# Two-block transformer kernel on one core: the last weight unit by blocks with its sums of squares taken early, down projections' and gates' low parts on VectorE alone, and a norm's next low part in two halves

## The chip, the cores and the metric

One core of one Trainium2 chip. The metric is device time in microseconds (us) of one launch. The time before is the median of three runs; one further execution was recorded by the hardware profiler, and every row below is from that one.

## The reference, cut to what matters

Two decoder blocks on 256 tokens (272 with 16 meta tokens) of width 1024, in float32. The first has two layers: attention with low-rank projections, then a mixer of window means, each followed by a feed-forward part with a causal convolution over 3 tokens. The second is gated linear attention with a short convolution, a gated feed-forward part, and a gate on a per-layer embedding. What matters here:

```python
def conv_ffn(h, w_up, conv_w, conv_b, w_down):
    u = h @ w_up                       # 1024 -> 2 x 2816
    u = conv_b + sum(conv_w[j] * up[:, j:j + L] for j in range(3))
    gate, val = jnp.split(u, 2, axis=-1)
    return (jax.nn.silu(gate) * val) @ w_down      # 2816 -> 1024
...
h = h + rmsnorm(f, norm_ffn_post[i])
...
        u2 = _rmsnorm(h, ln2_g[i])
        a, bb = jnp.split(u2 @ w_gate_upffn[i], 2, axis=-1)
        h = h + (jax.nn.silu(a) * bb) @ w_down[i]
        u3 = _rmsnorm(h, ln3_g[i])
        gate = jax.nn.sigmoid(u3 @ w_ple_gate[i])
        h = h + gate * (p[i] @ w_ple_proj[i])
    return _rmsnorm(h, lnf_g)
```

## The kernel before, in words

Activations lie transposed: the 1024 channels are 8 chunks of 128 partitions, tokens are the columns (272, 258 or 256 of them). Every float32 product is three matmuls of rounded parts, high x high, low x high and high x low (lines 441 to 443), which add up in one PSUM bank.

Weights come as a fixed list of units (`STREAM`). A unit is 16 to 24 tiles of 128x128 and yields 1 to 8 blocks of 128 output channels. Unit n uses slot n % 2 of three pairs of buffers: `raw` (filled by DMA on SyncE's queue), `wh` and `wl`. Its life is: SyncE loads `raw` when both low parts of unit n - 2 are written (`slot_free`); ScalarE copies raw to `wh` (`high`, lines 956 and 959) when TensorE is through with unit n - 2; then `wl` = raw - wh is made (`low`). VectorE makes the first `vector_cols(n)` columns (lines 1317 and 1323) and GpSimd, if `pool_share(n)`, the rest (line 1832), a quarter of the tiles rounded up. TensorE waits for all of it (`parts_ready`). Each engine runs its own list of instructions in order, written out by hand; semaphores tie them together.

Some units are made in two halves: `high(n, first=...)` and `low(n, first=...)` split at `first_half(n)`, half of VectorE's columns, and TensorE, given `first_low`, starts the unit on the first half and waits for the rest when it reaches it. During the last up units the second unit of a down projection is made so (on VectorE the order is first half, `x_low` of the last chunk of the hidden vector at line 1431, second half).

A norm works on sums of squares. ScalarE squares a chunk (line 977 or 967), GpSimd adds chunks into `acc` (line 1849), TensorE multiplies `acc` and the last one or two squares by a column of 1/1024 (lines 509, 512, 529: `norm_sums`, `chunk_sums`), a small chain on VectorE (or square root on ScalarE at line 983 and reciprocal at 1341) gives 1/rms, and TensorE spreads it over the partitions (line 543, `norm_rows`). Where a projection follows a norm, its first unit runs on values not yet divided, and the rows are spread in the middle of its second unit.

After each layer part `add_post` on VectorE adds the normed result to `h` chunk by chunk, makes the low part of the next operand (`u_low`, line 1332) and at the end calls `low(unit)` for the second weight unit that follows: one instruction over 2048 columns. TensorE is by then in the first unit of the next part.

The program's end: eight units `down2` (one block of 22 tiles each), then four units `pgate` (two blocks each). For each pair of blocks VectorE scales them by the rows out of PSUM (`scaled`, line 1379), ScalarE takes the sigmoid (line 1298), VectorE multiplies by the projected embedding (line 1810) and adds to `h` (line 1812), ScalarE squares `h` (line 977) and GpSimd adds squares 0 to 5. Then come the last norm (six plus two squares), eight VectorE products (line 1818) and four stores. `keep_busy` multiplies weights into a bank that nobody reads, to pass the time of a wait.

## Time and profile before

| what | us |
|---|---|
| median of three runs | 948.71 (945.36 to 949.46) |
| the profiled execution, its own time | 950.01 |
| its span, first to last instruction | 948.2 |
| TensorE matmul busy in it | 912.0 |
| VectorE, ScalarE, GpSimd busy in it | 681.7, 512.9, 276.4 |

Times in rows are us from the span's start. A row of the timeline has start, length, engine, line, operation and tiles; the bracket is the engine's idle time just before it and what ended it. "issue" there means that the profile names no releaser. A matmul's row is longer than the distance between two rows, since matmuls are pipelined.

### The profile page before, as it was taken

What the parts mean: (1) busy time and instruction counts of PE and PEld (TensorE: products, weight loads), DVE (VectorE), ACT (ScalarE), POOL (GpSimd) and SP (SyncE); (2) the same over time, 40 slices, a digit from 0 to 9 for tenths busy, and PEclk for the clock granted to TensorE, in tenths of its full rate; (3) what the DMA queues carried; (4) which work ended last, traced back from release to release, by engine and by line L of the source; (5) the groups of instructions that cost most, each with busy time, mean ns of one, the idle gap of its engine ahead of it and who ended that gap; (6) DMA issues with size and microseconds to landing.
All of it is one profiled execution on the core that took longest, in us unless ns stands there. A gap on an engine that the chain in (4) does not pass through costs nothing.

```text
span 948.2 us, 19994 instructions
## 1 busy us (share of the span) xinstructions
PE 912.0 (96%) x7354; PEld 884.7 (93%) x7354; DVE 681.7 (72%) x1168; ACT 512.9 (54%) x851; POOL 276.4 (29%) x202
## 2 busy tenths in 40 slices
PE   6999999999999999999999999999989999999996
PEld 6986798999999997899999999999989999999995
DVE  7767529999994225699999533889777888785666
ACT  5765656666655346566666544454455554454443
POOL 4118752000015534200000464200024334345633
PEclk9999999999999998799999999999999999999997
DMA  7541132544554531144445554354234555465431
GB/s 249 181 158 46 46 134 89 178 177 177 177 196 164 210 133 46 45 177 177 177 177 210 184 188 174 96 194 157 89 113 174 185 201 182 177 227 184 166 134 45
DMA packets 22147, 146.80 MB, mean 155 GB/s; under 512 B 2752, under 2 KB 5328, under 8 KB 6736
## 3 DMA queue, kind: packets, MB, share of 16 engines
q1 hardware_dynamic: 22096, 146.11, 43.1%
q8 instruction: 34, 0.56, 0.2%
q14 instruction: 17, 0.14, 0.0%
HBM read 143.94 MB, written 1.05 MB: 153 GB/s over the span
## 4 chain that ended last, share of the span: by engine, by line
PE 83%; DVE 10%; ACT 3%; issue 2%; POOL 1%; DMA 0%; POOLq 0%; SPq 0%; DVEq 0%; ACTq 0%
PE bank L441 23%; PE bank L442 23%; PE bank L443 23%; PE bank L681 2%; DVE u_low L1332 2%; ACT w_high L959 1%; DVE w_low L1323 1%; PE bank L529 1%; DVE h L1405 1%; PE bank L814 1%; DVE bank L1397 1%; PE bank L697 1%; PE bank L543 1%; PE bank L715 1%; PE bank L512 1%
## 5 line engine op out<-in xcount | busy, mean ns | idle before, releaser
L441 PE MATMUL bank<-u_high,w_high 128*128 128x256 f32 (+2 forms) x1400 | 401.7, 287 | 13.1 <-DVE u_low L1332 8.6
L442 PE MATMUL bank<-u_low,w_high 128*128 128x256 f32 (+2 forms) x1400 | 399.4, 285 | 0.0
L443 PE MATMUL bank<-u_high,w_low 128*128 128x256 f32 (+2 forms) x1400 | 398.2, 284 | 0.0
L1832 POOL TENSOR_TENSOR w_low<-raw,w_high 128x512 fp32r<-128x512 f32 (+1 forms) x60 | 168.8, 2814 | 463.0 <-ACT w_high L959 463.0
L1323 DVE TENSOR_TENSOR w_low<-raw,w_high 128x1024 fp32r<-128x1024 f32 (+5 forms) x119 | 198.1, 1664 | 125.7 <-ACT w_high L959 124.6
L441 PEld LDWEIGHTS bank<-u_high,w_high 128*128 128x128 f32 x1400 | 266.1, 190 | 15.5 <-DVE u_low L1332 8.1
L442 PEld LDWEIGHTS bank<-u_low,w_high 128*128 128x128 f32 x1400 | 265.8, 190 | 0.0
L443 PEld LDWEIGHTS bank<-u_high,w_low 128*128 128x128 f32 x1400 | 265.5, 190 | 0.0
L959 ACT ACTIVATE w_high<-raw 128x1024 fp32r<-128x1024 f32 (+5 forms) x119 | 195.2, 1640 | 73.2 <-PE bank L443 65.0
L441 PE MATMUL bank<-x_high,w_high 128*128 128x256 f32 (+1 forms) x608 | 173.9, 286 | 4.4 <-ACT x_high L1261 2.5
L443 PE MATMUL bank<-x_high,w_low 128*128 128x256 f32 (+1 forms) x608 | 173.3, 285 | 0.0
L442 PE MATMUL bank<-x_low,w_high 128*128 128x256 f32 (+1 forms) x608 | 172.7, 284 | 0.0
L441 PEld LDWEIGHTS bank<-x_high,w_high 128*128 128x128 f32 x608 | 115.3, 190 | 6.4 <-issue 3.3
L442 PEld LDWEIGHTS bank<-x_low,w_high 128*128 128x128 f32 x608 | 115.2, 189 | 0.0
L443 PEld LDWEIGHTS bank<-x_high,w_low 128*128 128x128 f32 x608 | 115.1, 189 | 0.0
L956 ACT ACTIVATE w_high<-raw 128x1024 fp32r<-128x1024 f32 (+1 forms) x66 | 65.7, 995 | 77.1 <-PE bank L443 73.6
L1454 DVE SCALAR_TENSOR_TENSOR conv_out<-conv_in,par,conv_out 128x272 f32<-128x272 f32 (+1 forms) x176 | 82.2, 507 | 7.6 <-ACT conv_out L1036 2.0
L1849 POOL TENSOR_TENSOR acc<-acc,sq 128x256 f32<-128x256 f32 (+1 forms) x51 | 45.0, 883 | 141.1 <-ACT sq L977 130.6
L1317 DVE TENSOR_TENSOR w_low<-raw,w_high 128x1024 fp32r<-128x1024 f32 (+1 forms) x66 | 75.5, 1143 | 12.2 <-ACT w_high L956 9.1
L1379 DVE TENSOR_TENSOR conv_in<-bank,r_rows 128x256 f32<-128x256 f32 (+2 forms) x140 | 54.1, 427 | 15.0 <-PE bank L443 9.6
L1043 ACT ACTIVATE conv_out<-conv_out 128x272 f32<-128x272 f32 (+1 forms) x44 | 18.7, 425 | 71.1 <-DVE conv_out L1454 71.1
L1036 ACT ACTIVATE conv_out<-conv_in,par 128x272 f32<-128x272 f32 (+1 forms) x88 | 48.1, 594 | 11.8 <-DVE conv_in L1379 10.7
(213 smaller groups left out, 1030.1 us busy)
## 6 DMA issues: line engine op xcount, KB each, us to landing
raw<-w_up_dram SPq DMA_DIRECT2D x66, 1024.0 KB, 4.8
raw<-w_down_dram SPq DMA_DIRECT2D x24, 1408.0 KB, 6.1
raw<-w_gin_c_dram SPq DMA_DIRECT2D x4, 1536.0 KB, 6.8
raw<-w_wo_dram SPq DMA_DIRECT2D x4, 1024.0 KB, 5.0
raw<-w_wout_dram SPq DMA_DIRECT2D x4, 1024.0 KB, 4.9
raw<-w_pgate_dram SPq DMA_DIRECT2D x4, 1024.0 KB, 4.7
raw<-w_gin_v_dram SPq DMA_DIRECT2D x2, 1024.0 KB, 4.7
raw<-w_gin_g_dram SPq DMA_DIRECT2D x2, 1024.0 KB, 6.2
```

The lines of the kernel that those rows point to most:

```text
L441: nc.tensor.matmul(out, hi, rhi, start=start, stop=False)
L442: nc.tensor.matmul(out, hi, rlo, start=False, stop=False)
L443: return nc.tensor.matmul(out, lo, rhi, start=False, stop=stop)
L956: nc.scalar.activation(wh[n % 2][:, 0:split], raw[n % 2][:, 0:split], ACT.Copy).then_inc(*S.step(first))
L959: nc.scalar.activation(wh[n % 2][:, split:cols], raw[n % 2][:, split:cols], ACT.Copy).then_inc(high_parts, 1)
L1036: nc.scalar.activation(cv[:, hf, 0:T], ur[:, hf, 2 + skip:2 + skip + T], ACT.Identity, bias=pcol(f"cb{l}", hf * FC + j), scale=pcol(f"cw{l ...
L1317: nc.vector.tensor_tensor(wl[n % 2][:, 0:split], raw[n % 2][:, 0:split], wh[n % 2][:, 0:split].bitcast(F32), ALU.subtract)\
L1323: nc.vector.tensor_tensor(wl[n % 2][:, split:cols], raw[n % 2][:, split:cols], wh[n % 2][:, split:cols].bitcast(F32), ALU.subtract).then_i ...
L1379: nc.vector.tensor_tensor(out, bank[BLOCKS[b]["bank"]][:, 0:T], rows[:, 0:T], ALU.mult)\
L1454: nc.vector.scalar_tensor_tensor(cv[:, hf, 0:T], ur[:, hf, skip + tap:skip + tap + T], pcol(f"cw{l}", (tap * 2 + hf) * FC + j), cv[:, hf, ...
L1832: nc.gpsimd.tensor_tensor(wl[n % 2][:, at], raw[n % 2][:, at], wh[n % 2][:, at].bitcast(F32), ALU.subtract).then_inc(low_parts_g, pool_cou ...
L1849: nc.gpsimd.tensor_tensor(acc[:, a, 0:T], acc[:, a, 0:T], x, ALU.add).then_inc(*step)
```

## The change

Five edits. (1) `pool_share` no longer holds for `down0`, `down1`, `down2` and `pgate`: VectorE makes their whole low part; `first_half` follows from the wider `vector_cols` (1408 columns of 2816 in place of 1024), and SyncE's queue writes four loads of each down projection out ahead of its loop instead of two. (2) `add_post` makes the next unit's low part in two instructions of 1024 columns with a signal each, and TensorE starts `up0`'s, `up1`'s and `gin`'s second unit on the first. (3) In the gates ScalarE makes the high part and VectorE the low part of the last unit one turn earlier, during the first pair of blocks. (4) The last unit runs block after block. In the middle of its second block TensorE takes the sum over squares 0 to 3; squares 4 to 7 are multiplied singly, from a buffer of their own each (`m`), so that GpSimd adds four squares instead of six; six unread matmuls stand before the last one and four after it. (5) In the last pair each block goes through scaling, sigmoid, product, addition and square by itself, and the table for the square root is loaded after the last square.

```diff
@@ -85,7 +85,8 @@
 PIECES = DC // 2
 
 
-SQUARES_IN_M = {"f0": T1, "a1": T1, "f1": SEQ + HISTORY, "g": SEQ}
+
+SQUARES_IN_M = {"f0": T1, "a1": T1, "f1": SEQ + HISTORY, "g": SEQ, "out": SEQ}
 
 OVER_D, OVER_Q, OVER_KV, OVER_HEAD = range(4)
 MEAN_OF = (D, QR, KVR, GDV)
@@ -143,8 +144,10 @@
 def pool_share(n):
 
 
-    return n == FIRST_UNIT["up0"] or UNITS[n]["name"] not in ("uqn", "uqr", "uk", "uv", "up0", "up1", "gin_k", "gin_v",
-                                                               "gin_g", "gin_c", "wout", "pproj")
+
+    return n == FIRST_UNIT["up0"] or UNITS[n]["name"] not in ("uqn", "uqr", "uk", "uv", "up0", "down0", "up1", "down1",
+                                                               "gin_k", "gin_v", "gin_g", "gin_c", "wout", "pproj",
+                                                               "down2", "pgate")
 
 
 def pool_counts(n):
@@ -366,7 +369,7 @@
                                 sp.dma_start(dst, src_).then_inc(tables_in, 16)
                 else:
 
-                    apart = 4 if not pool_share(n0 + 2) else 2 if units == DC or not pool_share(n0 - 1) else 0
+                    apart = 4 if not pool_share(n0 + 2) else 2 if not pool_share(n0 - 1) else 0
                     for u in range(apart):
                         slot_free(n0 + u, pool_share(n0 + u - 2))
                         sp.dma_start(raw[(n0 + u) % 2][:, 0:cols], src[u, :, :]).then_inc(loaded[(n0 + u) % 2], 16)
@@ -554,6 +557,12 @@
                     nc.tensor.matmul(bank[BLOCKS[b]["bank"]][:, 0:T1], wh[n % 2][:, 0:P], wh[n % 2][:, 0:T1],
                                      start=True, stop=True)
 
+            def spare_products(n, times):
+
+
+                for _ in range(times):
+                    nc.tensor.matmul(bank[2][:, 0:T1], wh[n % 2][:, 0:P], wh[n % 2][:, 0:T1], start=True, stop=True)
+
             def keep_busy_early(n):
 
 
@@ -585,7 +594,8 @@
                 us = (uh, ul)
                 unit(n0, T, us, high_then_low(sums_name))
                 norm_sums(sums_name, f"{sums_name} acc {DC - 2}", squares(0, T), True)
-                unit(n0 + 1, T, us, None, lambda: norm_rows(sums_name, token_rows(R_BANK, T)))
+                unit(n0 + 1, T, us, None, lambda: norm_rows(sums_name, token_rows(R_BANK, T)),
+                     first_low=f"{sums_name} next low" if l < 2 else None)
                 with pe.Fori(0, (FC - 2) // 2) as i:
                     for k in range(2):
                         unit(n0 + 2 + k, T, us, i=i)
@@ -855,7 +865,7 @@
             us = (uh, ul)
             unit(n, T, us, high_then_low("g"))
             norm_sums("g", f"g acc {DC - 2}", squares(0, T), True)
-            unit(n + 1, T, us, None, lambda: norm_rows("g", token_rows(R_BANK, T)))
+            unit(n + 1, T, us, None, lambda: norm_rows("g", token_rows(R_BANK, T)), first_low="g next low")
             pe.wait_ge(freed["v"], BLOCKS[FIRST_BLOCK["gin_a"]]["freed"])
             pe.wait_ge(tables_in, 16 * 7)
             for pair in range(2):
@@ -933,8 +943,13 @@
             norm_sums("e", f"e acc {DC - 2}", squares(0, T), True)
             unit(n + 1, T, us, None, lambda: norm_rows("e", token_rows(R_BANK, T)))
             unit(n + 2, T, us)
-            unit(n + 3, T, us)
-            norm_sums("out", f"out acc {DC - 3}", squares(0, T), True, late=(DC - 2, DC - 1))
+            blocks_in_turn(n + 3, T, lambda b, k: (uh[:, k, 0:T], ul[:, k, 0:T]), DC,
+                           middle=lambda: norm_sums("out", f"out acc {DC - 5}", squares(0, T), True, late=()))
+            for k in range(DC - 4, DC - 1):
+                chunk_sums("out", len(squares(0, T)), k)
+            spare_products(n + 3, 6)
+            last_sums("out", len(squares(0, T)))
+            spare_products(n + 3, 4)
             norm_rows("out", token_rows(R_BANK, T))
 
 
@@ -1290,17 +1305,29 @@
                 u_high("e", c, T, META, "ln3")
             for u in range(4):
                 n = FIRST_UNIT["pgate"] + u
-                if n + 2 < len(UNITS):
+                if u == 0:
                     high(n + 2)
-                for b in range(2):
+                def gate(b):
                     c = 2 * u + b
                     act.wait_ge(freed["v"], BLOCKS[FIRST_BLOCK["pgate"] + c]["freed"])
                     nc.scalar.activation(cv[:, b, 0:T], cv[:, b, 0:T], ACT.Sigmoid).then_inc(*S.step(f"ple gate {c}"))
-                if u == 3:
-                    load_table(ACT.Sqrt)
-                for c in range(2 * u, 2 * u + 2):
+
+                def out_square(b):
+                    c = 2 * u + b
                     act.wait_ge(*done(f"out h {c}"))
                     square("out", c, h[:, c, META:T1], T, S.step(f"out sq {c}"))
+                if u == 3:
+                    for b in range(2):
+                        gate(b)
+                        out_square(b)
+                else:
+                    gate(0)
+                    gate(1)
+                    if u == 0:
+                        high(n + 3)
+                    out_square(0)
+                    out_square(1)
+            load_table(ACT.Sqrt)
             rms("out", 2)
 
 
@@ -1408,7 +1435,12 @@
                         scale(c + 1)
                     if c > 1:
                         u_low(nxt, c - 1, T, t0, gain)
-                low(unit)
+
+                half, cols, at = first_half(unit), vector_cols(unit), unit % 2
+                dve.wait_ge(high_parts, unit + 1)
+                for cs, signal in ((slice(0, half), S.step(f"{nxt} next low")), (slice(half, cols), (low_parts_v, 1))):
+                    nc.vector.tensor_tensor(wl[at][:, cs], raw[at][:, cs], wh[at][:, cs].bitcast(F32), ALU.subtract)\
+                        .then_inc(*signal)
 
             def ffn_up(l, T, conv, name, skip=0):
 
@@ -1800,17 +1832,23 @@
             keep_rows("e", T)
             for u in range(4):
                 n = FIRST_UNIT["pgate"] + u
-                for b in range(2):
+
+                def gate_in(b):
                     scaled(cv[:, b, 0:T], FIRST_BLOCK["pgate"] + 2 * u + b, (freed["v"], 1), T)
-                if u == 1:
-                    low(n + 2)
-                for b in range(2):
+
+                def gated(b):
                     c = 2 * u + b
                     dve.wait_ge(*done(f"ple gate {c}"))
                     nc.vector.tensor_tensor(cv[:, b, 0:T], cv[:, b, 0:T], m[:, c, 0:T], ALU.mult).then_inc(*S.step())
                     dve.wait_ge(*S.now())
                     nc.vector.tensor_tensor(h[:, c, META:T1], h[:, c, META:T1], cv[:, b, 0:T], ALU.add)\
                         .then_inc(*S.step(f"out h {c}"))
+
+                for step, b in ((gate_in, 0), (gated, 0), (gate_in, 1), (gated, 1)) if u == 3 else \
+                        ((gate_in, 0), (gate_in, 1), (gated, 0), (gated, 1)):
+                    step(b)
+                if u == 0:
+                    low(n + 3)
                 dve.wait_ge(*S.now())
             norm("out", tiles_of(T))
             dve.wait_ge(*done("out rows"))
@@ -1840,7 +1878,7 @@
             def add_square(name, c, T, ready, a=0, k=None):
                 label = c if k is None else k
                 pool.wait_ge(*ready)
-                if name in SQUARES_IN_M:
+                if name in SQUARES_IN_M and name != "out":
 
                     pool.wait_ge(*done(f"{name} u low {c}"))
                 pool.wait_ge(*S.now())
@@ -1936,7 +1974,7 @@
             low(FIRST_UNIT["pgate"] + 2)
             low(FIRST_UNIT["pgate"] + 3)
             clear("e")
-            for c in range(DC - 2):
+            for c in range(DC - 4):
                 add_square("out", c, T, done(f"out sq {c}"))
```

## Rows read from the trace of the kernel before

**Rows 1.** The page: busy times of the engines.

```profile
PE 912.0 (96%) x7354; PEld 884.7 (93%) x7354; DVE 681.7 (72%) x1168; ACT 512.9 (54%) x851; POOL 276.4 (29%) x202
```

**Rows 2.** Busy time by stretch: the last down projection and the end, with its columns.

```profile
core 0: us, PE busy (x) PEld busy (x) DVE busy (x) ACT busy (x) POOL busy (x), PEclk, DMA share, GB/s
860.00:910.00 50.00, 50.00 (x425) 50.00 (x424) 29.43 (x20) 18.92 (x18) 30.80 (x14) 1.00 0.47 167
936.00:948.20 12.20, 3.91 (x18) 3.45 (x18) 5.53 (x15) 3.02 (x7) 0.73 (x1) 0.58 0.25 86
```

**Rows 3.** TensorE's timeline: second unit's first matmul behind the first and third norm.

```profile
154.39 0.37 PE L441 MATMUL bank<-u_high,w_high 128*128 128x272 f32 x1 [0.56 <-issue]
...
603.82 0.36 PE L441 MATMUL bank<-u_high,w_high 128*128 128x256 f32 x1 [0.50 <-issue]
```

**Rows 4.** VectorE's timeline: the low part behind the first of these norms.

```profile
151.43 2.85 DVE L1323 TENSOR_TENSOR w_low<-raw,w_high 128x2048 fp32r<-128x2048 f32 x1
```

**Rows 5.** Groups by line and shape: count, busy us and mean ns, idle before.

```profile
L1832 POOL TENSOR_TENSOR w_low<-raw,w_high 128x768 fp32r<-128x768 f32 x26 | 94.5, 3633 | 320.2 <-ACT w_high L959 320.2
L1323 DVE TENSOR_TENSOR w_low<-raw,w_high 128x2048 fp32r<-128x2048 f32 x33 | 77.8, 2358 | 89.4 <-ACT w_high L959 89.4
...
L1317 DVE TENSOR_TENSOR w_low<-raw,w_high 128x1024 fp32r<-128x1024 f32 x46 | 56.3, 1224 | 4.3 <-ACT w_high L956 1.2
```

**Rows 6.** TensorE's timeline: waits at the starts of the down projections.

```profile
298.71 0.39 PE L441 MATMUL bank<-x_high,w_high 128*128 128x272 f32 x1 [0.19 <-POOL w_low L1832]
...
530.67 0.36 PE L441 MATMUL bank<-x_high,w_high 128*128 128x256 f32 x1 [0.19 <-DVE x_low L1431]
...
534.20 0.36 PE L441 MATMUL bank<-x_high,w_high 128*128 128x256 f32 x1
...
539.94 0.38 PE L441 MATMUL bank<-x_high,w_high 128*128 128x256 f32 x1 [0.54 <-POOL w_low L1832]
...
847.40 0.36 PE L441 MATMUL bank<-x_high,w_high 128*128 128x256 f32 x1 [0.63 <-issue]
```

**Rows 7.** VectorE's and GpSimd's timelines at these starts.

```profile
530.10 0.42 DVE L1431 TENSOR_TENSOR x_low<-x_full,x_high 128x256 fp32r<-128x256 f32 x1
...
844.29 2.87 POOL L1832 TENSOR_TENSOR w_low<-raw,w_high 128x768 fp32r<-128x768 f32 x1 [4.25 <-ACT w_high L959]
```

**Rows 8.** Timelines at the start of the gates: VectorE, GpSimd, TensorE.

```profile
913.84 1.52 DVE L1332 SCALAR_TENSOR_TENSOR u_low<-h,par,u_high 128x256 fp32r<-128x256 f32 x1
...
912.21 2.87 POOL L1832 TENSOR_TENSOR w_low<-raw,w_high 128x512 fp32r<-128x512 f32 x1 [4.08 <-ACT w_high L959]
...
915.51 0.36 PE L441 MATMUL bank<-u_high,w_high 128*128 128x256 f32 x1 [0.45 <-DVE u_low L1332]
```

**Rows 9.** Timelines before the last unit: ScalarE, GpSimd, TensorE.

```profile
925.01 1.90 ACT L959 ACTIVATE w_high<-raw 128x2048 fp32r<-128x2048 f32 x1
...
926.99 2.85 POOL L1832 TENSOR_TENSOR w_low<-raw,w_high 128x512 fp32r<-128x512 f32 x1 [7.17 <-ACT w_high L959]
...
930.05 0.36 PE L441 MATMUL bank<-u_high,w_high 128*128 128x256 f32 x1 [0.78 <-issue]
```

**Rows 10.** Timelines of the end: VectorE and GpSimd beside each other, ScalarE, TensorE.

```profile
932.37 0.76 DVE L1379 TENSOR_TENSOR conv_out<-bank,r_rows 128x256 f32<-128x256 f32 x2
...
930.24 3.58 POOL L1849 TENSOR_TENSOR acc<-acc,sq 128x256 f32<-128x256 f32 x4
...
936.89 1.28 ACT L986 ACT_TABLE_LOAD   x1
...
940.65 0.17 ACT L983 ACTIVATE norm_t<-bank 128x2 f32<-128x2 f32 x1 [1.65 <-PE bank L529]
...
941.14 1.22 PE L543 MATMUL bank<-ident,norm_y 128*128 128x128 f32 x4 [0.53 <-DVE norm_y L1341]
```

**Rows 11.** Busy time by stretch, columns as in rows 2: around the second norm.

```profile
381.00:389.00 8.00, 8.00 (x43) 8.00 (x43) 3.41 (x10) 4.05 (x8) 1.06 (x2) 0.57 0.00 1
398.50:402.00 3.50, 3.50 (x17) 3.50 (x18) 3.26 (x10) 0.15 (x1) 0.00 (x0) 0.51 0.66 246
```

## The prediction, made before the change was timed

> **What bounds the kernel now.** I read the page's busy times first: TensorE is busy in 912.0 of 948.2 us, the others 682 at most [rows 1]. So only two things can move the end: how long TensorE waits, and the tail after its last product. In the stretches the reader sees that the last down projection has no waits at all, 425 matmuls in 50.0 us, 0.118 each, while from 936.0 to the end TensorE works 3.9 of 12.2 us [rows 2]. Then the timeline of TensorE for its waits, and the other engines' timelines around each wait for its cause. A wait costs more than its bracket: a full-rate matmul's row is 0.28 long but starts 0.12 after the one before, so idle time x costs x + 0.16, and the next row comes 0.1 late. I count x + 0.25 behind a product and x + 0.1 behind the short sums of a norm.
>
> **The norms' halves (edit 2).** The first product of the second unit waits 0.56 us behind the first norm, 0.58 behind the second, 0.50 behind the third [rows 3]. The bracket names nobody, but VectorE's low part of 2048 columns runs from 151.43 to 154.28 [rows 4], and TensorE starts 0.1 after it. It takes 2.85 where such a part takes 2.36 on average; an instruction of 1024 columns takes 1.22 [rows 5]. So the first half is ready at 151.43 + 0.5 + 1.2 = 153.2, before the sums end (about 153.8), and the wait is gone: (0.56 + 0.58 + 0.50) + 3 x 0.1 = 1.9 us. The second half is ready at about 154.35, and TensorE comes to it 24 matmuls later (3 us). The extra instruction costs VectorE under 0.1, which moves the norm's small chain by as much; its rows are asked for only in mid-unit. `up0` and `up1` then run with TensorE as the bound, and the third gain goes into a stage whose VectorE chain starts from the rows that TensorE spreads, so it starts earlier too. If it does not, 0.6 is lost: 1.3 to 1.9.
>
> **Low parts of the down projections (edit 1).** Removed: GpSimd's 768 columns, 3.63 us on average beside VectorE's 2.36 for 2048 [rows 5]. Added: VectorE does 2816. From 1.22 at 1024 and 2.36 at 2048 a column costs 1.1 ns, so 3.1 to 3.2 us. The unit's low part is then ready 0.5 us and more before, and at `down0` and `down1` these waits go: 0.19 + 0.25 = 0.4 (at 298.71); 0.54 + 0.25 = 0.8 (at 539.94) [rows 6]; at 534.20 the first half now reaches three chunks further, 0.3; a like one in `down0` 0.15. At 847.40 the row says "issue", but GpSimd's part ended at 844.29 + 2.87 = 847.16 [rows 7]. VectorE alone: its first half waits for ScalarE's longer one and ends about 844.3, then the hidden product, then 1408 columns (1.6) to about 846.5; TensorE is free at 846.6. The gain is 0.63 + 0.25 = 0.9; if VectorE is 0.3 late, 0.6. Against it: at `down0` and `down1` the first half on VectorE grows from 1024 to 1408 columns, +0.4 us, ahead of `x_low`, which ended at 530.52 [rows 7] and for which TensorE already waited (530.67, [rows 6]). That costs 0.4 in each, 0.8 together. ScalarE's longer first half is hidden by the wait for VectorE behind it. Sum: 0.15 (`down0`) + 0.7 (`down1`) + 0.9 = 1.8; between 1.2 and 2.6 (`x_low` hidden). In the units' middle nothing changes, as TensorE has no wait there [rows 2]; ScalarE 2.6 and VectorE 3.2 after a slot comes free make 6.0 of a unit's 66 x 0.118 = 7.8. SyncE's two more loads written out ahead of the loop wait for the same slots, which come free earlier: nothing. The squares that GpSimd adds come sooner: nothing.
>
> **Start of the gates (edit 1).** The last low part of `h` took 1.52 us instead of about 0.5 because GpSimd was at its 2.87 us part, and TensorE waited 0.45 [rows 8]. Now VectorE's part takes 2.3 from 912.17, then 0.5: ready at 914.9 instead of 915.36, and the wait costs 0.2 instead of 0.7. Gain 0.5.
>
> **Last unit earlier (edit 3).** TensorE waits 0.78 at 930.05, until GpSimd's part ended at 926.99 + 2.85; ScalarE had begun the high part at 925.01, behind two blocks' sigmoids and squares [rows 9], though TensorE had left that slot 48 x 0.118 = 5.7 before 929.3, at 923.6. Now (the old times less 0.5): high part 923.2 to 925.1, low part to 927.45, TensorE ready for it at 930.05 - 0.78 - 0.16 - 0.5 = 928.6. The stall, 1.0, is gone for TensorE. What is queued behind: VectorE's scaling of blocks 2 and 3, which frees the banks that the last unit needs now stands behind this low part; done at 927.9 and 928.2, before 928.6. That works because scaling reads PSUM: two of them took 0.76 with GpSimd's additions running beside [rows 10]. The Trainium skill says so too (SBUF — State Buffer, Who interferes with whom): a VectorE instruction with one SBUF input does not contend with GpSimd, one with two is fully blocked until the other has finished. The row agrees; if the scaling were blocked, the banks would come 0.8 later and 0.4 of the gain would be gone.
>
> **The tail (edits 4 and 5).** Now VectorE's chain decides, not TensorE, so I step through it from 927.45, with 0.42 a step on VectorE or ScalarE and 0.05 a hand-over. Blocks 2, 3: scaling 0.8, a block by GpSimd's second addition until 929.0, four steps, 930.7. Blocks 4, 5: scaling 0.8, sigmoid, 0.5 behind GpSimd, four steps, 933.9. Block 6: scaling, sigmoid, product, addition, 935.7. Block 7, whose product is long ready (TensorE ends at about 935.0, with 0.7 for the sums in the middle): scaling 936.1, sigmoid 936.55, two steps 937.5, square 937.9. Then the table, 1.28 as before [rows 10], which formerly ran beside VectorE's last products, now lies on the path: 939.3 with its small trial instruction. Sums of square 7 end at about 938.4, hidden, and so are the ten unread matmuls (1.3). The square root starts at 939.3 where it started at 940.65 [rows 10]: 1.35 gained from the gates' start to here, the 0.5 and what survives of the 1.0 in it. Spreading the rows took 1.22 at a mean clock of 0.58 [rows 2, 10]; at full clock it is about 0.6, so 0 to 0.6 more, of which I take none, because TensorE is idle for two stretches of a microsecond there now too. The eight products and four stores are unchanged. Bounds: 0.6 (GpSimd blocks four steps, not two) and 2.4.
>
> **Sum.** 1.9 + 1.8 + 1.35 = 5.05 us. Against the profiled execution, 950.01 (span 948.2 and 1.8 around it): 945.0. That execution lies 1.3 above the median of the three runs, so the median goes from 948.71 to 943.7, 0.53% less. Bounds: 3.1 to 6.9.
>
> **Rivals.**
> A, chance 0.18: TensorE's clock gives back more. Behind the second norm the clock was at its lower level (1.2 of 2.4 GHz) for 3.5 us and TensorE began 17 matmuls there where about 29 fit [rows 11]; before it TensorE had paced itself by `u_low` and then had the wait of rows 3. The norms before and after look alike and had no such stretch, so the removed 0.7 may be enough. Gain 1.5 more, and with full clock in the tail 2: 941.8. Against it: the longer drop before it, 8 us at 0.57, lies where nothing is changed [rows 11]. The Trainium skill (TensorE: Matmul & The Clock Gate, Part 1) says the halved rate is the default and activity lifts it, which would favour this rival; no row here shows a stall of that size deciding.
> B, 0.22: the end gives back its gain. Edit 3 puts 2.3 us of VectorE ahead of six blocks' work, and edit 5 puts the table behind the last square. If GpSimd's four additions each block VectorE for their full 0.9 us (3.58 for four, [rows 10]), the square root starts a microsecond later: gain 0.3 there, 4.0 in all, 944.7.
> C, 0.14: TensorE's removed waits in the norms or at the down projections return one step later (the third norm's in the `gin` stage, `x_low` 0.4 later than thought in both down projections): 1.4 less, 945.1; with B as well 946.2.
> D, 0.04, slower: clock drops move. One more long one (43 matmuls in 8 us where about 65 fit, [rows 11]) costs some 2.7; two eat the 5.05 and leave 949.1, three 951.8. It decides from the second. For it: one VectorE instruction less or more moves every later stretch, and the three runs already span 4.1 us. Against it: every edit makes TensorE denser but the last one.
> E, 0.02: the change does nothing, since the waits are replaced one by one: 948.7.
> My forecast as worked out: 0.40.
>
> **How the numbers follow.** 0.5% of 948.71 is 4.7 us, about what a measurement of this kernel can tell from no change; the line is at 944.0. The forecast lies 0.3 past it, so its 0.40 split 0.30 faster and 0.10 same; A is faster, 0.18; B and C mostly same, 0.06 of their 0.36 faster; D slower in 0.03 of 0.04, E same. Faster 0.54, same 0.43, slower 0.03. The range takes A at its far end (941.8 less 1.3 for the spread of the runs) and C with B at the other (946.2 with 0.8): 940.5 to 947.0.
>
> **What would show it.** Right: no idle row of TensorE behind the norms; none at the second and third unit of `down1` or at the start of `down2`; the wait for `x_low` in `down1` at 0.6 instead of 0.19, and a new one in `down0`; low parts of 2816 columns at 3.1 to 3.2 us; TensorE going into the last unit without a wait; the chain of waits ending over VectorE's steps, the table load, the square root. Wrong: a wait for a free bank at the last unit, a wait for GpSimd's fourth sum in the middle of it, or TensorE waiting for the second half at the third chunk of the second unit.

## The result, and the profile after

| | before | changed |
|---|---|---|
| median, us | 948.71 (945.36 to 950.51, 5 runs) | 939.38 (937.44 to 940.41, 5 runs) |
| profiled execution, span | 948.2 | 938.6 |

The medians differ by 9.3 us. The ratio is 0.9895 (95% interval 0.9872 to 0.9918); it is an estimate over all runs, here and below, and not the quotient of the two medians. The forecast was 943.7 with a range from 940.5, so the sign was right and the size was too small by almost half.

The page of the changed kernel, its busy times and the granted clock in 40 slices:

```profile
PE 909.2 (97%) x7372; PEld 883.9 (94%) x7372; DVE 684.6 (73%) x1172; ACT 512.1 (55%) x851; POOL 191.6 (20%) x172
...
PEclk9999999999999998899999999999999999999998
```

TensorE's busy time falls by 2.8 us although it runs 18 matmuls more; GpSimd loses 85 us of work and VectorE gains 3 [rows 1]. A fall in busy time with more matmuls points to the clock. Busy time by stretch behind the first and the second norm (columns as in [rows 2]):

```profile
152.00:159.00 7.00, 7.00 (x60) 6.96 (x60) 6.63 (x16) 2.33 (x5) 0.33 (x1) 1.00 0.45 152
...
395.00:398.50 3.50, 3.50 (x31) 3.45 (x31) 3.22 (x12) 1.64 (x2) 0.33 (x1) 1.00 0.24 56
```

Behind the second norm TensorE has 31 matmuls in 3.5 us at full clock, where before it had 17 at half [rows 11]. TensorE's timeline: first matmul of the second unit behind the first norm, the last chunk of `down1`'s first unit, and the second unit behind the third norm:

```profile
153.42 0.39 PE L444 MATMUL bank<-u_high,w_high 128*128 128x272 f32 x1
...
525.71 0.29 PE L446 MATMUL bank<-x_high,w_low 128*128 128x256 f32 x1
526.01 0.36 PE L444 MATMUL bank<-x_high,w_high 128*128 128x256 f32 x1
...
596.86 0.37 PE L444 MATMUL bank<-u_high,w_high 128*128 128x256 f32 x1
```

None of these rows has a bracket, as those of [rows 3, 6] had; only the last chunk of `down1`'s first unit starts 0.30 behind its neighbour instead of 0.12, and there TensorE had waited in [rows 6] too. In the stages around `down0` and `down2` no matmul starts more than 0.2 behind the one before. VectorE at the start of the gates and before the last unit:

```profile
904.33 2.29 DVE L1350 TENSOR_TENSOR w_low<-raw,w_high 128x2048 fp32r<-128x2048 f32 x1 [1.58 <-ACT w_high L974]
906.54 0.48 DVE L1359 SCALAR_TENSOR_TENSOR u_low<-h,par,u_high 128x256 fp32r<-128x256 f32 x1
...
917.35 2.29 DVE L1350 TENSOR_TENSOR w_low<-raw,w_high 128x2048 fp32r<-128x2048 f32 x1 [1.29 <-ACT w_high L974]
```

`u_low` takes 0.48 instead of 1.52 [rows 8]. The last unit's low part finds VectorE idle for 1.29 us in front of it. ScalarE at the end:

```profile
929.25 0.42 ACT L982 ACTIVATE m<-h 128x256 f32<-128x256 f32 x1 [0.95 <-DVE h L1844]
929.68 1.28 ACT L1001 ACT_TABLE_LOAD   x1
930.97 0.20 ACT L1001 ACTIVATE warm<-ident 128x1 f32<-128x1 f32 x1
931.08 0.15 ACT L998 ACTIVATE norm_t<-bank 128x2 f32<-128x2 f32 x1
```

The table load stands on the path, as forecast.

**Where the 9.6 us of the span went.** I cut each trace at the starts of the same high parts on ScalarE (a fixed list of instructions) and compared the pieces. "Start" runs from the span's start to the third high part, "end" from the third last one to the span's end; pieces that differ by 0.1 or less everywhere are left out.

| piece | before | changed | gain |
|---|---|---|---|
| start | 10.9 | 10.6 | 0.3 |
| first norm and first turns of `up0` | 16.6 | 16.0 | 0.6 |
| `up0` to `down0` | 32.6 | 31.5 | 1.1 |
| second norm and first turns of `up1` | 33.2 | 31.1 | 2.1 |
| `up1` to `down1` | 31.8 | 30.2 | 1.6 |
| end of `down1`, third norm, first units of `gin` | 31.4 + 30.2 | 31.2 + 29.1 | 1.3 |
| `up2` to `down2` | 26.7 | 25.8 | 0.9 |
| end | 38.0 | 36.3 | 1.7 |

The start is not the change's: no edit touches it, and it takes 10.0 to 10.9 in the profiles of this document, 10.0 in a run whose code is there the same as before.

### The profile page after: what moved, and what is told of

It reads as the page before. It is cut to its first block, busy times and chain, and to the rows that moved or that the text cites. A ratio compares the mean times of both kernels' runs of the same rounds, so it can differ in the third digit from the quotient of the medians.

```text
span 938.6 us, 19945 instructions
## 1 busy us (share of the span) xinstructions
PE 909.2 (97%) x7372; PEld 883.9 (94%) x7372; DVE 684.6 (73%) x1172; ACT 512.1 (55%) x851; POOL 191.6 (20%) x172
## 4 chain that ended last, share of the span: by engine, by line
PE 86%; DVE 8%; ACT 3%; issue 1%; DMA 1%; SPq 0%; DVEq 0%; ACTq 0%
PE bank L444 24%; PE bank L445 24%; PE bank L446 24%; PE bank L691 2%; PE bank L532 1%; PE bank L824 1%; ACT w_high L974 1%; DVE u_low L1359 1%; PE bank L707 1%; DVE h L1432 1%; DVE bank L1424 1%; PE bank L546 1%; PE bank L482 1%; DVE w_low L1350 1%; PE bank L515 1%
## 5 line engine op out<-in xcount | busy, mean ns | idle before, releaser
L1350 DVE TENSOR_TENSOR w_low<-raw,w_high 128x1024 fp32r<-128x1024 f32 (+6 forms) x115 | 205.7, 1788 | 112.2 <-ACT w_high L974 111.2
L1887 POOL TENSOR_TENSOR acc<-acc,sq 128x272 f32<-128x272 f32 (+1 forms) x45 | 53.2, 1181 | 511.7 <-ACT sq L992 502.1
L971 ACT ACTIVATE w_high<-raw 128x1024 fp32r<-128x1024 f32 (+2 forms) x66 | 67.5, 1023 | 72.8 <-PE bank L446 69.2
L1870 POOL TENSOR_TENSOR w_low<-raw,w_high 128x512 fp32r<-128x512 f32 (+1 forms) x32 | 70.6, 2206 | 141.7 <-ACT w_high L974 141.7
L1344 DVE TENSOR_TENSOR w_low<-raw,w_high 128x1024 fp32r<-128x1024 f32 (+2 forms) x66 | 77.9, 1180 | 13.4 <-ACT w_high L971 10.9
L1486 DVE SCALAR_TENSOR_TENSOR conv_out<-conv_in,par,conv_out 128x272 f32<-128x272 f32 (+1 forms) x176 | 79.2, 490 | 7.5 <-ACT conv_out L1051 2.0
```

The source lines that it names most:

```text
L971: nc.scalar.activation(wh[n % 2][:, 0:split], raw[n % 2][:, 0:split], ACT.Copy).then_inc(*S.step(first))
L1344: nc.vector.tensor_tensor(wl[n % 2][:, 0:split], raw[n % 2][:, 0:split], wh[n % 2][:, 0:split].bitcast(F32), ALU.subtract)\
L1350: nc.vector.tensor_tensor(wl[n % 2][:, split:cols], raw[n % 2][:, split:cols], wh[n % 2][:, split:cols].bitcast(F32), ALU.subtract).then_i ...
L1486: nc.vector.scalar_tensor_tensor(cv[:, hf, 0:T], ur[:, hf, skip + tap:skip + tap + T], pcol(f"cw{l}", (tap * 2 + hf) * FC + j), cv[:, hf, ...
L1870: nc.gpsimd.tensor_tensor(wl[n % 2][:, at], raw[n % 2][:, at], wh[n % 2][:, at].bitcast(F32), ALU.subtract).then_inc(low_parts_g, pool_cou ...
L1887: nc.gpsimd.tensor_tensor(acc[:, a, 0:T], acc[:, a, 0:T], x, ALU.add).then_inc(*step)
```

## The experiments

Before each stands what was expected of it. Times are medians; the pieces are those of the table. "The root" is the square root of the last norm. The kernel before was run beside each group: 947.74, 947.75 and 948.92.

**One low part behind the norms again.** Edit 2 undone:

```diff
-                half, cols, at = first_half(unit), vector_cols(unit), unit % 2
-                dve.wait_ge(high_parts, unit + 1)
-                for cs, signal in ((slice(0, half), S.step(f"{nxt} next low")), (slice(half, cols), (low_parts_v, 1))):
-                    nc.vector.tensor_tensor(wl[at][:, cs], raw[at][:, cs], wh[at][:, cs].bitcast(F32), ALU.subtract)\
-                        .then_inc(*signal)
+                low(unit)
```

and `first_low` taken from the three second units.

> The changed kernel with edit 2 alone undone: the low part behind a norm is one instruction of 2048 columns again, and TensorE waits for all of it. The forecast's term: 1.9 us slower than the changed kernel (941.3), by waits of 0.5 to 0.6 us at three places. Theory (the removed wait behind the second norm also kept TensorE's clock up there): 3.4 slower (942.8) in executions in which a stretch at the lower clock follows the second norm, and such a stretch is in the profile. Rival (the three gains are lost again one stage later): no slower than 939.4, with the three waits there but an equally long idle time gone elsewhere.

943.04 (6 runs), 3.7 over the changed kernel; ratio to before 0.9934 (0.9908 to 0.9961). Its busy times by stretch, behind the second and behind the first norm:

```profile
397.20:400.60 3.40, 3.40 (x19) 3.40 (x18) 2.87 (x6) 0.00 (x0) 0.00 (x0) 0.50 0.88 308
154.80:158.20 3.40, 3.40 (x17) 3.40 (x16) 2.92 (x6) 0.00 (x0) 0.00 (x0) 0.51 0.89 306
```

Both stretches are at the lower level, 1.2 GHz. The piece of the second norm is 33.2 again against 31.1: by the run with the wait filled, below, 0.6 of the 2.1 is the wait and 1.5 the clock. The rival, gains lost again one stage later, falls.

**GpSimd's share back in the down projections.** Edit 1 undone for `down0`, `down1` and `down2` (the three names taken out of the list in `pool_share`):

> The changed kernel with edit 1 undone for the three down projections alone: GpSimd makes 768 of 2816 columns again. Forecast's term: 1.8 us slower (941.2): waits of 0.4, 1.1 and 0.9 back, x_low 0.4 sooner in two places. Theory (GpSimd's 2.8 us part in the last up turns blocks VectorE's taps, which makes x_low later, not sooner): 3.3 slower (942.7), x_low of the last chunk some 1.2 us later than in the changed kernel and a tap of about 2.1 us instead of 0.5 in the turn before. Rival (the gain behind the up units is the clock's): under 1 slower.

942.46 (8 runs), 3.1 over the changed kernel; ratio to before 0.9932 (0.991 to 0.9955). The pieces are 32.7, 31.8 and 26.7 against 31.5, 30.2 and 25.8: 3.7 us, twice the forecast's 1.8. The rival (the gain is the clock's, under 1 us) falls. Why, in three timelines of the last turn but one of `up0`. Before, GpSimd and VectorE:

```profile
278.22 2.81 POOL L1832 TENSOR_TENSOR w_low<-raw,w_high 128x768 fp32r<-128x768 f32 x1 [126.08 <-ACT w_high L959]
...
279.25 2.08 DVE L1454 SCALAR_TENSOR_TENSOR conv_out<-conv_in,par,conv_out 128x272 f32<-128x272 f32 x1
```

The changed kernel, VectorE:

```profile
277.43 1.62 DVE L1350 TENSOR_TENSOR w_low<-raw,w_high 128x1408 fp32r<-128x1408 f32 x1
278.97 0.50 DVE L1486 SCALAR_TENSOR_TENSOR conv_out<-conv_in,par,conv_out 128x272 f32<-128x272 f32 x1
```

This experiment, VectorE:

```profile
278.63 2.08 DVE L1485 SCALAR_TENSOR_TENSOR conv_out<-conv_in,par,conv_out 128x272 f32<-128x272 f32 x1
```

A tap of the convolution (one multiply-add over a chunk) takes 2.08 us where 0.50 is its length: it starts in the middle of GpSimd's 2.81 us part and ends 0.3 after it. Counted from the start of the piece, `x_low` of the last chunk but one then starts 0.9 us later than in the changed kernel in both `down0` and `down1`, and that of the last chunk 0.5 later, not the 1.2 expected: VectorE's shorter first half gives some of it back. At `down2` GpSimd's part blocks `x_low` itself, 2.06 us instead of 0.42 in both last turns. That is the rule of exclusive access that the prediction cites for the last unit (the Trainium skill, SBUF — State Buffer, Who interferes with whom: of two such instructions the later one is blocked until the other has finished). This trace agrees with it within 0.2 us: 1.6 us of block behind a part that had 1.8 to run.

**The end undone.** Edits 3, 4 and 5 taken back, the gates' low parts still on VectorE:

> The changed kernel with edits 3, 4 and 5 undone: the last unit's parts one turn later, both blocks together, sums at the end, table load ahead of the last squares; the gates' low parts stay on VectorE. Forecast's term, 1.35 less the 0.5 of the gates' start: 0.85 slower (940.3). Theory (as the changed kernel's trace reads, 1.8 from the gates' start on, 0.5 of it from the start): 1.3 slower (940.7). Rival (the low part on VectorE alone already gives the last unit in time): TensorE goes into the last unit with a wait under 0.3 and the time is 0.5 slower or less.

938.69 (6 runs), no slower than the changed kernel at 939.38 (0.9898, 0.9871 to 0.9925, beside 0.9895). The rival holds. VectorE's low part of the last unit and TensorE behind it:

```profile
915.72 2.29 DVE L1333 TENSOR_TENSOR w_low<-raw,w_high 128x2048 fp32r<-128x2048 f32 x1 [1.50 <-ACT w_high L969]
...
923.70 0.28 PE L446 MATMUL bank<-u_high,w_low 128*128 128x256 f32 x1
...
926.81 0.37 PE L532 MATMUL bank<-mean_weights,sq 128*128 128x1 f32 x1 [1.83 <-ACT sq L987]
```

The low part ends at 918.01 and TensorE goes into the last unit at 918.1 with no idle row: VectorE's 2.29 us are in time even one turn later, if only by 0.1, and only GpSimd's 2.85 had been late [rows 9]. The end piece is 36.5 against 36.3 (0.3 before rounding). In this profile the clock fell just before the last norm's sums; what that hides is under "The gates' low parts alone".

**Down projections alone.** The kernel before with only the three `down` names added to `pool_share`'s list:

> The kernel before with only the low parts of the three down projections given to VectorE. Forecast's term: 1.8 us faster than before (946.9). Theory (VectorE no longer blocked by GpSimd in the last up turns): 3.3 faster (945.4). Rival (the parts depend on each other, and alone this one only moves the wait to x_low): no faster than before by 0.5. The half-clock stretch behind the second norm should still be in the profile by the theory on the clock, as the wait there is still made.

945.07 (12 runs): 0.9971 (0.995 to 0.9992), 2.7 faster. In the profile the three pieces are 31.5, 30.2 and 25.8, as in the changed kernel, 3.6 together. The two pieces behind `down1` and around the third norm are 31.2 and 29.8 instead of 31.4 and 30.2: another 0.6 that this edit alone gives. A half-clock stretch of 3.4 us stands behind the second norm, as expected, and one behind the first.

**A down projection's first half at 1024 columns.**

```diff
-            return vector_cols(n) // P // 2 * P
+            return 8 * P if UNITS[n]["name"].startswith("down") else vector_cols(n) // P // 2 * P
```

> The changed kernel with the first half of a down projection's low part at 1024 columns, as before, and all of it still on VectorE. It measures the cost that the forecast put at 0.4 us in each of the first two down projections: VectorE's first half 1.22 instead of 1.62 us, x_low of the last chunk 0.4 earlier. If TensorE waits for x_low in the changed kernel, its start of the down projection is 0.4 shorter in each (0.8 in all); if not, as its trace reads (one start 0.18 late, in down1, none in down0), the gain is 0.1 to 0.25 in down1 and nothing in down0, and the time is 939.2 beside 939.4.

939.71 (4 runs), 0.9916 (0.9885 to 0.9947): no difference. The pieces are 31.5 and 30.2 as in the changed kernel. The last `x_low` starts 0.27 sooner than in the changed kernel and nothing is gained by it. So the 0.4 us that the forecast put on each of two starts is not there: `x_low` has room.

**The last unit in two halves.** `high(n + 3, first="last first high")` on ScalarE and `low(n + 3, None, "last first high")` on VectorE:

> The changed kernel with the last unit's high and low parts in two halves, so that VectorE starts 0.9 us sooner on it and is through 0.8 sooner. If VectorE's list is what sets the end from there on, the stretch from the last high part to the end is 0.5 to 0.8 shorter (bounded by TensorE's last product, which VectorE then meets earlier). Rival (the table load and the sums set it): no shorter by more than 0.1.

937.82 (4 runs), 0.9899 (0.9867 to 0.9931). To compare ends without the clock I count from the first matmul that spreads the rows of the gates' norm. The last low part ends at 7.0 instead of 7.8 and block 6 is added 0.8 sooner, but the last addition to `h` ends at 17.2 instead of 17.3 and the square root starts at 19.1 instead of 19.2. The rival's number holds (no more than 0.1), by a cause that it did not name: TensorE's last product ends at 15.4 in both and now bounds the last block.

**The last unit's parts in their old turn.** Edit 3 undone, 4 and 5 kept:

```diff
-                if u == 0:
+                if n + 2 < len(UNITS):
                     high(n + 2)
...
-                    if u == 0:
-                        high(n + 3)
```

and on VectorE `low(n + 2)` in the second turn, between scaling and products.

> The changed kernel with edit 3 alone undone: the last unit's parts one turn later, as before, with edits 4 and 5 kept. Theory, from the run with all three undone (the end took 36.5 us from the third last high part on, against 36.3): edit 3 costs 0.7, because VectorE stands idle for 1.3 us in front of a high part that cannot come sooner, with two blocks' scaling behind it, and edits 4 and 5 gain 0.9. So this one ends 0.4 to 0.7 sooner than the changed kernel, 35.7 in that stretch, and TensorE goes into the last unit with a wait under 0.2. The forecast's view (edit 3 removes a wait of 1.0): a wait of 0.8 to 1.0 in front of the last unit and the end 0.3 or more later.

937.97 (6 runs), 0.9899 (0.9873 to 0.9925). Counted as above, the fourth block is added at 10.3 instead of 10.8, so edit 3 does cost VectorE 0.5 there, but the square root starts at 19.1 instead of 19.2, and the end piece is 36.2; TensorE has no idle row in front of the last unit. The wait of 0.8 to 1.0 that the forecast's view asks for does not come; my 0.4 to 0.7 does not come either, for the bound is again TensorE's last product at 15.4, which the sums in the middle of the unit put 0.65 later than without them (14.7).

**The norms' waits filled.** Edit 2 undone and, for the first two norms, added work: five matmuls that nobody reads between the sums and the second unit.

```diff
+                if l < 2:
+                    pe.wait_ge(high_parts, n0 + 2)
+                    for _ in range(5):
+                        nc.tensor.matmul(bank[3 * (n0 % 2) + 2][:, 0:T1], wh[(n0 + 1) % 2][:, 0:P],
+                                         wh[(n0 + 1) % 2][:, 0:T1], start=True, stop=True)
```

> The changed kernel with edit 2 undone and, at the first two norms, five matmuls that nobody reads in the wait between the sums and the second unit (added work: TensorE is busy there and the second unit starts no sooner). Theory on the clock: the waits still cost 0.6 us each, but no stretch at the lower clock follows the first or the second norm, so the stage behind the second norm takes 31.7 us instead of 33.2 (31.1 with edit 2 in place) and that behind the first is never 1.5 longer. Rival (the lower clock came from something else, such as VectorE's later instructions): the stage takes 33.2 and the half-clock stretch is there.

941.18 (8 runs), 0.9935 (0.9912 to 0.9957). Busy times behind the second and behind the first norm:

```profile
396.50:400.00 3.50, 3.50 (x32) 3.45 (x31) 3.26 (x9) 2.45 (x4) 0.33 (x2) 1.00 0.13 19
154.00:157.50 3.50, 3.50 (x18) 3.50 (x18) 3.23 (x12) 0.37 (x1) 0.06 (x1) 0.51 0.61 206
```

Behind the second norm the clock stays up and the piece is 31.7, as expected (the wait kept, the clock not lost): the wait is 0.6 of the 2.1 and the clock 1.5. Behind the first norm the stretch at the lower level is there all the same. Half of the expectation fails, so filling the wait is not sufficient.

**The table ahead of the last square.** The run with edit 3 undone, and `load_table(ACT.Sqrt)` moved between the last sigmoid and the last square:

> Edit 3 undone and edits 4 and 5 kept, as in the run before, and the table for the square root loaded between the last sigmoid and the last square. Counted from the first matmul that spreads the rows of the gates' norm, the square root starts at 19.1 us there. If the table load lies on the path behind the last square, it starts 0.3 to 0.5 sooner, at 18.6 to 18.8. Rival (the last square then waits for the table and the sums come later by as much): at 19.1 again.

938.23 (4 runs), 0.9901 (0.9879 to 0.9924). The square root starts at 18.85 instead of 19.1: 0.25, a little under the expectation.

**The end together.** That, with the last unit's parts in halves in their old turn, three unread matmuls instead of six, and the sums over squares 0 to 3 behind the unit:

```diff
-            blocks_in_turn(n + 3, T, lambda b, k: (uh[:, k, 0:T], ul[:, k, 0:T]), DC,
-                           middle=lambda: norm_sums("out", f"out acc {DC - 5}", squares(0, T), True, late=()))
+            blocks_in_turn(n + 3, T, lambda b, k: (uh[:, k, 0:T], ul[:, k, 0:T]), DC)
+            norm_sums("out", f"out acc {DC - 5}", squares(0, T), True, late=())
```

> All that the runs point to at the end: edit 3 undone, the last unit's parts in two halves in their turn, the sums over squares 0 to 3 after the last unit and not in its middle (0.65 us less ahead of the last product), three unread matmuls instead of six, the table ahead of the last square. The square root starts at 18.0 to 18.3 us from the rows of the gates' norm, against 19.2 in the changed kernel, and the end is 0.9 to 1.2 sooner: some 938.3 beside 939.4. If VectorE's list for the earlier blocks still holds it back, under 0.5.

937.71 (5 runs), 0.9899 (0.988 to 0.9917). ScalarE's timeline:

```profile
925.60 1.28 ACT L1001 ACT_TABLE_LOAD   x1
926.89 0.20 ACT L1001 ACTIVATE warm<-ident 128x1 f32<-128x1 f32 x1
927.00 0.40 ACT L982 ACTIVATE m<-h 128x256 f32<-128x256 f32 x1
928.09 0.17 ACT L998 ACTIVATE norm_t<-bank 128x2 f32<-128x2 f32 x1 [0.70 <-PE bank L532]
```

The table load is hidden beside VectorE's last two steps and the square root starts at 18.15, 1.06 sooner than in the changed kernel; the end piece is 35.4 against 36.3. By the root this end is the best of all here; by the medians (interval of the ratio inside that of the changed kernel) it can't be told from it.

**Norms' halves alone.** The kernel before with edit 2:

> The kernel before with edit 2 alone. Theory: no stretch at the lower clock behind the first and the second norm, the stage behind the second takes 31.1 us instead of 33.2, and those behind the first and third are 0.6 to 0.7 shorter: 3.4 us in all, 4.9 where before had a stretch behind the first norm too: 944 to 945.5. The forecast's term alone, 1.9: 946.8.

944.51 (10 runs), 0.996 (0.9945 to 0.9976), 4.4 faster; the piece of the second norm 31.1, no stretch at the lower level behind either norm.

**The gates' low parts alone.** The kernel before with `pgate` added to the list:

> The kernel before with only the gates' low parts given to VectorE. Theory: the wait of 0.78 us in front of the last unit goes by this alone, not by moving the low part: the square root starts at 19.5 us from the rows of the gates' norm instead of 20.4, and the last low part of h is 0.5 sooner: 1.4 in all, 947.3. The forecast had 0.5 for it and gave the wait to edit 3.

947.9 (10 runs), 0.9982 (0.9971 to 0.9994), 1.0 faster where 1.4 were expected. The wait in front of the last unit is gone, and the square root starts at 18.8 instead of 20.4; in the run with the end undone, with the same instructions there, it starts at 19.5. The two differ by the clock at which the last eight small sums run. TensorE's rows of these sums, in the kernel before and in the run with the halves alone, which has the same instructions there too:

```profile
938.75 1.86 PE L529 MATMUL bank<-mean_weights,sq 128*128 128x1 f32 x8 [1.04 <-ACT sq L977]
...
931.96 1.05 PE L529 MATMUL bank<-mean_weights,sq 128*128 128x1 f32 x8 [1.05 <-ACT sq L978]
```

The lower level sets in at 17.6 in the first and at 19.5 in the second, and the root starts at 20.4 and at 19.6. So at the lower level the gates' low parts move the root from 20.4 to 19.5, at full clock from 19.6 to 18.8: 0.8 to 1.0 at equal clock. In the changed kernel and the four runs with its end the sums are done before the table is, and the root starts at 19.2 in all five. Beside the gates' low parts alone, edits 3 to 5 thus gain 0.3 where the clock falls before the sums and lose 0.4 where it stays up.

The three parts alone multiply to 0.9971 x 0.996 x 0.9982 = 0.9913; the whole gives 0.9895. Nothing shows that they need each other; the other 0.2% is within the intervals.

## Why the prediction fell short, step by step

**Norms' halves: the wait right, the clock missed.** The removed waits were sized at 1.9 and measure 0.6 at each of the first two norms and 0.7 at the third, 1.8 before rounding (the second from the run with the wait filled, the third against the runs without halves, 29.8). But the sum stopped there, and the clock, left to rival A at 0.18, is what came on top. A stretch at the lower clock stands behind the second norm in all four profiles that have neither halves nor filling, and in none of the nine with halves; behind the first norm in three of the four, and in none of the nine. Each costs 1.5 or more (33.2 less 31.7 with the wait filled; the piece that holds the first takes 153.3 to 153.9 in the four profiles that have it and 151.7 to 151.9 in the ten that do not). The step that failed is the sum for the norms itself, "(0.56 + 0.58 + 0.50) + 3 x 0.1 = 1.9 us": it prices the waits and puts the clock that follows them at nothing. I had the one stretch in the row and left it to a rival, because a longer drop lies where nothing is changed; that drop stayed, and the one behind the second norm went. The one profile of before could not show the cost at the first norm, as that execution happened to have no stretch there.

**Down projections: mis-sized, 3.6 instead of 1.8.** `down2` was right, 0.9 for 0.9. For the other two I had 0.15 and 0.7, measured 1.1 and 1.6. The step that failed is "that costs 0.4 in each": the run with 1024 columns shows no cost. I had added 0.4 us to VectorE ahead of `x_low` and had not asked what GpSimd's part takes from VectorE in the turn before: 1.6 us in one tap, removed by the same edit. The signs that I named for it, a wait of 0.6 for `x_low` in `down1` and a new one in `down0`, did not come: it is 0.18 in `down1` and nothing in `down0`. I had used that very mechanism for `u_low` at the gates, where TensorE's row named it, and not where the row named `x_low`. The waits themselves were counted short: in these two stages of before, the matmuls that start over 0.2 behind their neighbour are late by 0.9 and 1.8 us in all, in the changed kernel by 0 and 0.2. That is 2.5 of the 2.7, where I had 1.65; left out were one of 0.28 at 522.77 and several of 0.1.

**Start of the gates: right.** 0.5 forecast; `u_low` at 0.48 instead of 1.52, TensorE without an idle row.

**Last unit and tail: sum near, parts wrong.** I forecast 1.35, and the piece gives 1.7 in the profile. The square root starts at 19.2 from the norm's rows instead of 20.4, which is 1.2 beside the 0.5 in front. But 0.8 of this 1.2 is the clock at the eight small sums of before (20.4 against 19.6), which I had not in view: at full clock the changed kernel gains 0.4 there. And edit 3 was given the wait of 0.78, which the gates' low parts on VectorE remove by themselves. VectorE's step list was close: I had 11.85 us from the last low part's end to the square root, and it was 11.4. I had the 0.7 for the sums in the middle of the last unit, and called its last product "long ready"; it ends 0.65 later than without them, 0.2 before VectorE comes to it, and is the bound as soon as VectorE is faster. From the root to the end it takes 7.55 us instead of 7.57, so the "I take none" for the spreading of the rows was right.

**Rivals.** A came behind the second norm; by itself it gives 941.8, and the measured 939.4 needs the down projections' term as well. B (the end gives back its gain) came in part: not through GpSimd, whose additions delayed VectorE twice, by 0.5 and 0.4, about as forecast, but by the table load on the path and the middle sums: at full clock the gates' low parts alone have the root at 18.8, edits 3 to 5 at 19.2. C did not come; D and E did not.

**The range.** Between the two profiled executions 9.6 us went where I had 5.05. Of the 4.5 missing, 1.8 is the down projections' term, 1.5 the clock behind the second norm, 0.35 the end and 0.3 the start, which no edit touches. The other 0.6, behind `down1` and around the third norm, is the down projections' edit too, by the run with that edit alone; the forecast had nothing for it, and how it comes about was not followed up. The far end of the range took in A alone. (By their own terms A is 941.7 and C with B 946.1, not 941.8 and 946.2; nothing turns on it.) With the down term at its own upper bound (0.8 more) it would have been 939.7, still short: that bound was too tight as well.

## What to carry to other kernels

When an engine's share of work is taken away, look for every instruction of the engine that shares access with it and is longer than its usual length during that share, not only for the ones that end a wait. Price a removed wait by its idle row and by the stretch at the lower clock that may follow it, and look at several executions for such stretches before calling one of them an exception. Moving a part earlier is worth nothing if the slower of its two makers has been removed already: try the edits one by one, and compare two profiles of an end only where the clock fell at the same point of it. GpSimd's share blocks VectorE in the changed kernel still: in 19 turns of `up2` `x_low` takes 1.5 us beside GpSimd's 2.06 us part, where TensorE does not wait for it.

## What the runs showed of the hardware

The spread of one kernel's runs goes with TensorE's clock. The kernel before was timed 55 times beside the experiments, from 944.28 at a mean granted clock of 0.992 to 951.72 at 0.980, and the two go together almost on a line. At 0.992 the changed kernel takes 937.4 and 938.1 where before takes 944.3 to 945.5, at 0.986 it takes 940.4 where before takes 948.0 to 949.4: 7 to 8 us at equal clock. That the rest of the 9.3 is less time at the lower level fits this, but is not shown apart. Part of the spread lies where no edit reaches: near 357 us the lower level lasts 3.4 us in some profiles and 6.9 in others of different edits, and near 381 us three of the 14 have none. The end has this spread too: with the same instructions behind the gates the end piece is 36.3 in the changed kernel and 35.8 in the run with the first half at 1024 columns, where the lower level came later.

What sets the lower level is left open. It followed norms in which TensorE had paced itself by `u_low` and then waited 0.56 us; five filling matmuls kept it away behind one norm and not behind the other. The Trainium skill (TensorE: Matmul & The Clock Gate, Part 1) calls the halved rate the default that activity lifts; the runs agree in direction, and no run here shows how much activity it takes.
